# First-layer modulation as columns in the transposed copies, reordered loads, warmed roots, and a closing group by halves

## The chip, the cores and the metric

The kernel is one launch on one core of a Trainium2 chip. The metric is the device time in microseconds of that core. Three runs of the kernel before gave a median of 2481.85 us (2481.49 to 2483.36). All arithmetic is in float32.

PE is the tensor engine, DVE the vector engine, ACT the scalar (activation) engine, POOL the engine that issues the indirect gathers and the small loads, and SP the engine that issues nearly all the other loads. Each engine works its own instructions off in order and waits on semaphores.

## The reference

Two layers are computed over 256 latent tokens and 256 context tokens of width 1024. Layer 0 mixes tokens with multi-head latent attention (8 heads), layer 1 with grouped-query attention. After each mixer stands a PEER sub-layer: each token picks 16 of 16384 experts in each of 8 heads and takes their rows out of two tables. Cut to what matters here:

```python
for i in range(DEPTH):
    mod   = jax.nn.silu(c)     @ p['ada_w'] + p['ada_b']   # six parts of 1024
    mod_c = jax.nn.silu(c_ctx) @ p['ada_w'] + p['ada_b']
    h  = modulate(rmsnorm(x,  p['norm_mix']), sh_a,  sc_a)  # h * (1 + scale) + shift
    hc = modulate(rmsnorm(xc, p['norm_mix']), csh_a, csc_a)
    y, y_c = mixers[i % N_MIXERS](h, hc, *p['mixer'], need_ctx=need_ctx)
    x = x + g_a * y
    h = modulate(rmsnorm(x, p['norm_ffn']), sh_f, sc_f)
    x = x + g_f * peer_ffn(h, *p['peer'])
    if need_ctx: ...            # the same for the context, in layer 0 alone
return rmsnorm(x, norm_out)

# peer_ffn, a token and a head:
v1, i1 = top_k(s1, 16); v2, i2 = top_k(s2, 16)          # two lists of 128 keys
top_s, top_pos = top_k(v1[:, None] + v2[None, :], 16)   # of the 256 sums
expert = i1[pos // 16] * 128 + i2[pos % 16]
out += softmax(top_s) * gelu(t . u_tab[expert]) * v_tab[expert]
```

## The kernel before, in words

**Tiling.** A chunk is 128 tokens on the 128 partitions; chunks 0 and 1 are the context, 2 and 3 the latents. A *unit* is one chunk with one expert head. Layer 0 has 32 units (`FIRST`), layer 1 has 16. A unit has 16 gathers (L582), each of which brings for every token of the chunk one expert's row of both tables: 128 x 8 KB, 1 MB. DVE computes the dot product with the first half of a row (L2021), ACT applies Gelu and builds scaled diagonal matrices (L1256, L1553), and PE adds up the second halves through those diagonals into banks 0 to 3 of the accumulators (L1092). Units are worked in groups of four slots. The ring has 7, later 10, 12 and 15 slots. The rest of the latents' layer 0 (`lat`) is spliced between the groups at fixed positions.

**The opening.** Before the first gather, the context goes through the first attention and the modulation vectors of both layers are computed. The modulation weights are 48 pieces of 1 MB (`ada`); PE uses each with products into bank 0 (L141). Eight pieces make a *round*. The result of a round is 2 rows (latent and context) in each of four 32-partition groups; DVE adds the bias and folds in the norm gains (`ada_rows`, L1595 and L1607), POOL stores the rows in DRAM (L136), and where they are needed they are loaded again, broadcast over 128 partitions. For the first attention that is L545 (context) and L551 (latents), and `norm_rows` (L1611, L1612) scales and shifts a chunk by those rows before PE transposes it (`transposes`, L598) and ACT copies the transposed chunk out of the bank (`row_copies`, L1128). Then comes the input projection in two halves for each chunk (`in_half`, L603), and a loop over the 8 heads of the context (`ctx_proj`, `ctx_scores`, `ctx_transposes`, `ctx_values`), ten *turns* in all, each ended by three `ada` pieces. The output projection (`out_ctx`, L765) needs the weights `w_o_first`, which lie on slots 0 to 3 of the `ada` pieces; so the pieces from 35 on go through three slots only (`ada_place`, L274), one of which is the latent half of `hT`. Then follow the FFN norm, the first expert queries (L638), the scores, the two top-16 lists and `choose`, which ends with the indices of the first gather.

**Order of loads.** SP issues its loads in program order; a load into a slot in use waits for `ada_used`, and every later load waits behind it.

**The close of a chunk.** When the last group of a chunk's 8 units has been added up, DVE and ACT copy the four banks out (`add_output`, L1794 and L1795, and `copy_accumulators`), and DVE adds the result to x. That happens six times; behind the one at the end of layer 0 and the one at the end of the kernel no group follows at once.

**Roots.** Norms on ACT are a Square with accumulation and a Sqrt; the Sqrt needs a table load when Exp or Gelu came before (L1206, L1489).

## Time and profile before

| | |
|---|---|
| median of three runs | 2481.85 us |
| profiled execution, its time | 2484.57 us |
| profiled execution, its span | 2482.8 us |
| PE busy | 1669.9 us (67%) |
| DVE busy | 1587.5 us (64%) |
| ACT busy | 837.0 us (34%) |
| POOL busy | 922.7 us (37%) |
| gathers (software queue) | 811.23 MB, 79.4% of 16 engines' span |
| other loads and stores (hardware queue) | 119.50 MB, 13.0% |
| ACT table loads of the two largest groups | 86.0 and 61.6 us |

The span is from the first to the last instruction; the time of the same execution is 1.8 us longer. A busy share is an average over stages that are bound by different things, so the table says little by itself. The view in 40 slices of 62 us shows where the stages lie: slices 1 to 4 are the opening, slices 27 to 30 hold the end of layer 0 and the second attention, and all the others are units. "PEclk" is the granted clock of PE. The timeline lists instructions in order of time, with the idle time of the engine in front of each and what ended it; "x32" means that so many were merged in one row, and a float32 product appears there as two.

### The profile page before, as it was taken

The page shows a single profiled execution, that of the slowest core. Times are in us where ns is not written, and L with a number is a line of the kernel's source. Part 1 is how long each engine was busy: PE and PEld are TensorE (multiplying, and loading weights), DVE is VectorE, ACT ScalarE, POOL GpSimd, SP SyncE. Part 2 cuts the span into 40 slices and gives each one's busy share as a digit, 9 for nine tenths or more (in the row PEclk, how much of TensorE's full clock was granted, in tenths as well). Part 3 has the DMA queues.
Part 4 walks back from the last instruction along what each step waited for, and adds up shares of the span by engine and source line. Part 5 has one row for each costly group of instructions (what it writes and reads, how often), then busy time and mean ns, then how long its engine had stood idle before and what let it go on. Part 6 is the DMA issues. An engine that isn't in the chain of part 4 may idle for free. (4 is left out here: it accounts for less than half of the span.)

```text
span 2482.8 us, 27305 instructions
## 1 busy us (share of the span) xinstructions
PE 1669.9 (67%) x9121; PEld 727.2 (29%) x9121; DVE 1587.5 (64%) x3775; ACT 837.0 (34%) x2504; POOL 922.7 (37%) x836
## 2 busy tenths in 40 slices
PE   2988777777767667576755655568877565555554
PEld 0553543333324323232211211124543221111111
DVE  1132576788866667777777666544579687766654
ACT  1220334344452332434333433223333333332322
POOL 2010234444434444444444444410135444444440
PEclk8998898888888888888867867878989887777686
DMA  9895879999999999999999999982389999999995
GB/s 367 306 353 183 318 300 382 414 417 417 414 416 417 363 419 419 419 419 419 420 421 421 421 421 421 419 353 81 136 336 418 419 421 421 421 421 421 421 421 225
DMA packets 164974, 932.48 MB, mean 376 GB/s; under 512 B 16913, under 2 KB 51505, under 8 KB 60257
## 3 DMA queue, kind: packets, MB, share of 16 engines
q0 software_dynamic: 113392, 811.23, 79.4%
q1 hardware_dynamic: 51296, 119.50, 13.0%
q8 instruction: 72, 1.18, 0.2%
q14 instruction: 70, 0.57, 0.1%
q10 hardware_dynamic: 144, 0.01, 0.0%
HBM read 929.52 MB, written 1.15 MB: 375 GB/s over the span
## 5 line engine op out<-in xcount | busy, mean ns | idle before, releaser
L1092 PE MATMUL bank<-arena,aux 64*64 64x512 f32 x6144 | 989.8, 797 | 682.7 <-ACT aux L1553 653.3
L582 POOL DMA_INDIRECT arena<-in_uv,small x768 | 890.4, 1159 | 1331.6 <-PE bank L1092 959.8
L2021 DVE CUSTOM_DVE_ANT_0 arena<-arena,h 128x1024 f32<-128x1024 f32 x768 | 924.9, 1224 | 504.5 <-DMA arena<-in_uv,small 481.1
L1092 PEld LDWEIGHTS bank<-arena,aux 64*64 64x64 f32 x6144 | 281.6, 178 | 1337.3 <-ACT aux L1553 771.4
L1546 ACT ACTIVATE small<-small 128x4 f32<-128x4 f32 x192 | 39.3, 205 | 1201.4 <-DVE small L2021 1186.4
L1256 ACT ACTIVATE aux<-small 128x64 f32<-128x64 f32 x768 | 204.4, 336 | 8.9
L1553 ACT ACTIVATE aux<-aux,small 128x64 f32<-128x64 f32 x768 | 204.3, 336 | 6.5 <-issue 0.2
L638 PE MATMUL bank<-hT,aux 128*128 128x256 f32 (+1 forms) x768 | 170.2, 380 | 2.8 <-ACT hT L1128 2.8
L638 PEld LDWEIGHTS bank<-hT,aux 128*128 128x128 f32 x768 | 140.3, 203 | 49.0 <-issue 29.4
L1242 ACT ACT_TABLE_LOAD x67 | 86.0, 1283 | 1.2
L141 PE MATMUL bank<-arena,aux 128*32 128x512 f32 x312 | 48.3, 725 | 32.0 <-DMA arena<-in_ada 23.1
L136 POOL DMA_DIRECT2D mod_rows<-aux x24 | 12.1, 512 | 145.8 <-DVE aux L1607 90.1
L2021 DVE DVE_READ_ACCUMULATOR2_ANT small<- 128x1 f32 x768 | 62.9, 82 | 0.0
L1246 ACT ACT_TABLE_LOAD x48 | 61.6, 1283 | 0.8
L603 PE MATMUL bank<-arena,hT 128*128 128x384 f32 x128 | 45.5, 514 | 1.7 <-ACT arena L1295 1.1
L624 PE MATMUL bank<-arena 128*128 128x256 f32 x192 | 44.8, 383 | 0.9 <-ACT h L1320 0.9
L598 PE MATMUL bank<-ident,h 128*128 128x128 f32 x112 | 17.6, 308 | 39.9 <-DVE h L1612 39.9
L1755 DVE TENSOR_TENSOR aux<-small 128x256 f32<-128x256 uint32 x96 | 40.7, 424 | 4.7
L1757 DVE TENSOR_TENSOR aux<-aux,small 128x256 f32<-128x256 f32 x96 | 40.8, 426 | 3.3
L1758 DVE TENSOR_REDUCE small<-aux 128x16 f32<-128x256 f32 x96 | 40.3, 420 | 3.3
L1726 DVE MAX8 aux<-bank 128x8 f32<-128x128 f32 x84 | 25.0, 297 | 25.2 <-PE bank L646 11.4
L1123 ACT ACTIVATE h<-x 128x1024 f32<-128x1024 f32 x16 | 16.7, 1046 | 70.5 <-DVEq L1716 44.3
(224 smaller groups left out, 1519.3 us busy)
## 6 DMA issues: line engine op xcount, KB each, us to landing
arena<-in_ada SPq DMA_DIRECT2D x39, 1024.0 KB, 9.0
aux<-in_w_query SPq DMA_DIRECT2D x44, 512.0 KB
arena<-in_uv,small POOLq DMA_INDIRECT x768
hT<-in_ada SPq DMA_DIRECT2D x9, 1024.0 KB, 12.0
arena<-in_w_uq SPq DMA_DIRECT2D x16, 384.0 KB, 14.5
arena<-in_w_qkv SPq DMA_DIRECT2D x3, 2048.0 KB, 12.0
arena<-in_w_o SPq DMA_DIRECT2D x1, 4096.0 KB, 13.4
arena<-in_w_o SPq DMA_DIRECT2D x2, 2048.0 KB, 15.6
```

Source lines behind the costliest of these rows:

```text
L141: last = self.nc.tensor.matmul(bank[s * Q:(s + 1) * Q, :], self.cs[:, k, :], weights[:, 2 * s:2 * s + 2, :], start=(k == 0), stop=(k == KD ...
L582: nc.gpsimd.indirect_dma_start(out=ring[:, pos, :], out_offset=None, in_=d["uv"][unit // FIRST], in_offset=bass.IndirectOffsetOnAxis(ap=se ...
L603: last = nc.tensor.matmul(b[:, 0:HALF], hT[:, k, c * P:(c + 1) * P], self.w_in[:, k, half * HALF:(half + 1) * HALF], start=(k == 0), stop= ...
L624: last = nc.tensor.matmul(b[:, half * 256:half * 256 + 256], wq_head[:, k, half * P:half * P + P], cT[:, k, at:at + 256], start=(k == 0), ...
L638: last = nc.tensor.matmul(Q_BANK[:, side * 256 + at:side * 256 + at + width], weights[:, k, :], hT[:, k, lo:lo + width], start=(k == 0), s ...
L1092: last = nc.tensor.matmul(bank[2 * r + m][out:out + 64, :], self.dg[rr, (s + o) % 8, :], ring[rr, at, cols], start=first, stop=last_one)
L1242: nc.scalar.activation(self.warm, self.iota[:, 0:1], ACT.Gelu).then_inc(warmed, 1)
L1246: nc.scalar.activation(self.gate[:, m % 4, :], self.top, ACT.Exp, bias=self.nb, accum_out=self.es).then_inc(gate_done, 1)
L1256: last = nc.scalar.mul(self.gid[:, k, :], self.ident2, self.gate[:, m % 4, g * GRP + k:g * GRP + k + 1])
L1553: nc.scalar.mul(self.dg[:, s % 8, :], self.gid[:, k % GRP, :], self.w[:, n % 2, k:k + 1]).then_inc(diag_ready, 1)
L1757: link(nc.vector.tensor_tensor(self.OH, self.OH, self.indf[:, side, :].unsqueeze(1).broadcast_to([P, TOPK, TOPK]), ALU.mult))
L2021: last = nc.vector.tensor_tensor_reduce(out=ring[:, at, 0:D], in0=ring[:, at, 0:D], in1=h[:, c * D:(c + 1) * D], scale=1.0, scalar=0.0, op ...
```

## The change

1. **First attention's scale and shift as columns.** Chunks are only multiplied by their reciprocal root (ACT, `first_rows`), and transposed. The finished rows of round 0 are transposed on PE in four pieces, the useful columns are copied to `M0`, and the copies of the transposed chunks apply scale and shift per partition: four columns of a chunk on ACT (`first_copies`), four on DVE. The loads of these rows (L545, L551) and the four calls of `norm_rows` are gone. The latents' chunks are scaled in turn 4 of the head loop and copied by ACT, eight columns each, in the first units.
2. **Rows on two partitions.** Bias and gain rows are loaded to 2 partitions of each group instead of 32; the tiles are set to zero first.
3. **Loads reordered.** x comes in two halves, the latent half behind the first two heads' weights. `w_in` and `w_o` come by columns, in halves with a semaphore each. The first 8 `ada` pieces have a slot each. `w_o` is loaded after piece 28 instead of 34, when piece 25 has been used.
4. **PE's order.** Turns 8 and 9 of the loop use two pieces each, and the last six pieces are used between the output projections. The second half of chunk 1's output goes to bank 7 instead of bank 0.
5. **One-hot work at once.** `choose` handles both sides in three operations of 512 elements instead of six of 256.
6. **The closing group by halves.** In the last group of a chunk PE waits for all four diagonals and adds the first 512 output columns of all four slots, signals `closed`, then the other 512. The copies of the first half wait for `closed` alone.
7. **Warmed roots.** A Sqrt of a dummy tile stands ahead of the waits of four norms: the one behind layer 0's last chunk, layer 1's two FFN norms, and the last output norm.

The core of the diff:

```diff
-            eng.dma_start(rows[s * Q:(s + 1) * Q], bias[s].broadcast_to([Q, 512])).then_inc(loaded, 16)
+            eng.dma_start(rows[s * Q:s * Q + 2], bias[s].broadcast_to([2, 512])).then_inc(loaded, 16)
...
         def ada_place(n):
 
-            return n % 7 if n < 35 else 4 + (n - 35) % 3
+            return n if n < 8 else (n - 8) % 7 if n < 29 else 4 + (n - 29) % 3
...
+                sp.dma_start(x[:, CC:], d["tokens"][:, CC:]).then_inc(x_lat_loaded, 16)
...
-                    if n == 34:
-                        sp.wait_ge(ada_used, 32)
-                        sp.dma_start(self.w_o_first, d["w_o0"]).then_inc(w_o_loaded, 16)
+                    if n == 28:
+                        sp.wait_ge(ada_used, 26)
+                        for i in range(2):
+                            sp.dma_start(self.w_o_first[:, :, 512 * i:512 * i + 512], d["w_o0"][:, :, 512 * i:512 * i + 512]).then_inc(w_o_loaded[i], 16)
...
+                pe.wait_ge(rows_done, 1)
+                for j in range(4):
+                    last = nc.tensor.transpose(bank[1][:, j * P:(j + 1) * P], rows[0][:, j * P:(j + 1) * P], ident[:])
+                last.then_inc(m0_done, 1)
+                pe.wait_ge(nt_copied, 4)
+                pe.wait_ge(nt_moved, 4)
...
-                    for n in range(18 + 3 * u, 21 + 3 * u):
+                    for n in range(14 + 3 * u, 17 + 3 * u) if u < H else range(22 + 2 * u, 24 + 2 * u):
                         ada(n)
...
+                            closing = n % H == H - 1 and g == NG - 1
+                            pe.wait_ge(diag_ready, s + 2 + 2 * (closing and half == 0))
...
+                            if closing and half == 0:
+                                last.then_inc(closed, 1)
+                            else:
+                                last.then_inc(slots_free, 2 if closing else 1)
...
+                def first_copies(c, banks, ks):
+
+                    for k in ks:
+                        act.wait_ge(nt_done, 2 * c + k // 4 + 1)
+                        nc.scalar.activation(hT[:, k, c * P:(c + 1) * P], banks[k // 4][:, k % 4 * P:k % 4 * P + P], ACT.Identity,
+                                             bias=first_column(c, 0, k), scale=first_column(c, 1, k)).then_inc(nt_copied, 1)
...
+                for c, b in ((0, bank[6]), (1, bank[4])):
+                    for k in range(4, KD):
+                        dve.wait_ge(nt_done, 2 * c + 2)
+                        nc.vector.tensor_scalar(hT[:, k, c * P:(c + 1) * P], b[:, k % 4 * P:k % 4 * P + P],
+                                                first_column(c, 1, k), first_column(c, 0, k), ALU.mult, ALU.add).then_inc(nt_moved, 1)
...
                 def copy_accumulators(c):
                     for m in range(2):
+                        act.wait_ge(slots_free, (c + 1) * H * TOPK // 2) if m else act.wait_ge(closed, c + 1)
...
+                copy_accumulators(len(ORDER) - 1)
+                warm_sqrt()
                 out_norm(5, 3)
```

Three places of the order follow, in which the lines of the kernel after are its own. On PE, from the first `ada` product to the second transposes of projected rows, the kernel before has:

```order
L141 MATMUL bank<-arena,aux 32x512 x24
L141 MATMUL bank<-hT,aux 32x512 x4
L141 MATMUL bank<-arena,aux 32x512 x4
L598 MATMUL bank<-ident,h 128x128 x8
L603 MATMUL bank<-arena,hT 128x384 x16
L598 MATMUL bank<-ident,h 128x128 x8
L141 MATMUL bank<-arena,aux 32x512 x8
L603 MATMUL bank<-arena,hT 128x384 x16
L609 MATMUL bank<-ident,aux 128x128 x6
```

and the kernel after:

```order
L141 MATMUL bank<-arena,aux 32x512 x24
L605 MATMUL bank<-ident,h 128x128 x8
L141 MATMUL bank<-hT,aux 32x512 x4
L605 MATMUL bank<-ident,h 128x128 x8
L141 MATMUL bank<-arena,aux 32x512 x4
L695 MATMUL bank<-ident,aux 128x128 x4
L610 MATMUL bank<-arena,hT 128x384 x32
L141 MATMUL bank<-arena,aux 32x512 x8
L616 MATMUL bank<-ident,aux 128x128 x6
```

Both chunks are now transposed (L605) among the products of round 0, the rows of round 0 are transposed (L695) behind them, and the four halves of the projection (L610) stand together. On PE, the end of the head loop (`ctx_values`, L745) and the output projection (L765), before:

```order
L141 MATMUL bank<-arena,aux 32x512 x4
L745 MATMUL bank<-aux,arena 128x256 x2
L141 MATMUL bank<-arena,aux 32x512 x4
L141 MATMUL bank<-hT,aux 32x512 x4
L141 MATMUL bank<-arena,aux 32x512 x4
L765 MATMUL bank<-arena,hT 128x512 x24
L598 MATMUL bank<-ident,h 128x128 x8
```

and after (L760 and L782):

```order
L760 MATMUL bank<-aux,arena 128x256 x2
L141 MATMUL bank<-hT,aux 32x512 x4
L141 MATMUL bank<-arena,aux 32x512 x4
L782 MATMUL bank<-arena,hT 128x512 x16
L141 MATMUL bank<-arena,aux 32x512 x4
L141 MATMUL bank<-hT,aux 32x512 x4
L141 MATMUL bank<-arena,aux 32x512 x4
L782 MATMUL bank<-arena,hT 128x512 x8
L141 MATMUL bank<-arena,aux 32x512 x4
L141 MATMUL bank<-hT,aux 32x512 x4
L141 MATMUL bank<-arena,aux 32x512 x4
L605 MATMUL bank<-ident,h 128x128 x8
```

Six pieces moved behind the first two output projections. On SP, the loads around w_o, before:

```order
L400 DMA arena<-in_ada 128x2048 x3
L405 DMA arena<-in_w_uq 128x3x256
L406 DMA arena<-in_w_uk 128x2x128
L400 DMA hT<-in_ada 128x8x256
L442 DMA arena<-in_w_o 128x8192
L400 DMA arena<-in_ada 128x2048 x2
L400 DMA hT<-in_ada 128x8x256
```

and after:

```order
L410 DMA arena<-in_ada 128x2048
L410 DMA hT<-in_ada 128x8x256
L454 DMA arena<-in_w_o 128x8x512 x2
L410 DMA arena<-in_ada 128x2048
L415 DMA arena<-in_w_uq 128x3x256
L416 DMA arena<-in_w_uk 128x2x128
L410 DMA arena<-in_ada 128x2048
L410 DMA hT<-in_ada 128x8x256
```

The last head's weights (`w_uq`, `w_uk`) now follow w_o instead of preceding it, and nineteen pieces come behind it where thirteen did.

## Rows read from the trace of the kernel before

**Rows 1.** The page, 40 slices: ACT's busy tenths, and GB/s of all transfers.

```profile
ACT  1220334344452332434333433223333333332322
GB/s 367 306 353 183 318 300 382 414 417 417 414 416 417 363 419 419 419 419 419 420 421 421 421 421 421 419 353 81 136 336 418 419 421 421 421 421 421 421 421 225
```

**Rows 2.** The page, costliest groups: busy us, mean ns, idle before with its releaser.

```profile
L2021 DVE CUSTOM_DVE_ANT_0 arena<-arena,h 128x1024 f32<-128x1024 f32 x768 | 924.9, 1224 | 504.5 <-DMA arena<-in_uv,small 481.1
```

**Rows 3.** Timeline, start to first projection: start, us, engine, what, idle before.

```profile
31.91 1.93 PE L141 MATMUL bank<-hT,aux 128*32 128x512 f32 x8 [1.05 <-DMA hT<-in_ada]
34.39 1.81 PE L141 MATMUL bank<-arena,aux 128*32 128x512 f32 x8 [0.55 <-DMA arena<-in_ada]
37.10 0.69 DVE L1607 SCALAR_TENSOR_TENSOR aux<-aux 64x512 f32<-64x512 f32 x1
55.57 1.28 DVE L1611 SCALAR_TENSOR_TENSOR h<-x,small,arena 128x1024 f32<-128x1024 f32 x1 [17.78 <-DMA arena<-mod_rows]
60.88 13.44 PE L603 MATMUL bank<-arena,hT 128*128 128x384 f32 x32 [0.68 <-ACT hT L1128]
```

**Rows 4.** The timeline, second pair of projections to the head loop.

```profile
76.98 10.59 PE L603 MATMUL bank<-arena,hT 128*128 128x384 f32 x32
88.15 2.78 PE L141 MATMUL bank<-arena,aux 128*32 128x512 f32 x24
104.80 2.75 PE L624 MATMUL bank<-arena 128*128 128x256 f32 x12
```

**Rows 5.** The timeline, two starts of a turn, and the release of w_o.

```profile
135.25 0.69 PE L726 MATMUL bank<-aux 128*128 128x256 f32 x2
144.65 0.70 PE L726 MATMUL bank<-aux 128*128 128x256 f32 x2
153.31 0.33 SPq L442 DMA_DIRECT2D arena<-in_w_o  x1
```

**Rows 6.** The head loop's end: timeline, SP's waits, a window, DMA issues.

```profile
155.97 8.01 SPq L400 DMA_DIRECT2D arena<-in_ada  x2
210.42 22.35 PE L765 MATMUL bank<-arena,hT 128*128 128x512 f32 x48
...
SPq L400 <- PE bank L141: 109.1, 35, 15.3
...
175.00:180.00 5.00, 5.00 (x34) 3.23 (x37) 0.00 (x0) 1.47 (x6) 0.00 (x0) 1.00 0.37 149
...
hT<-in_ada SPq DMA_DIRECT2D x9, 1024.0 KB, 12.0
```

**Rows 7.** The timeline, transposes for the first query, and the first gather.

```profile
233.02 1.09 PE L598 MATMUL bank<-ident,h 128*128 128x128 f32 x8 [0.25 <-DVE h L1612]
251.36 1.02 POOL L582 DMA_INDIRECT arena<-in_uv,small  x1 [36.80 <-DVEq L1762]
```

**Rows 8.** The page, costliest groups: one of the one-hot operations.

```profile
L1755 DVE TENSOR_TENSOR aux<-small 128x256 f32<-128x256 uint32 x96 | 40.7, 424 | 4.7
```

**Rows 9.** The timeline, four column copies on ACT in the second layer.

```profile
1679.07 1.50 ACT L1421 ACTIVATE hT<-bank,small 128x128 f32<-128x128 f32 x4 [2.28 <-PE bank L598]
```

**Rows 10.** The timeline, second attention: query rows, a table load, two transposes.

```profile
1664.60 14.00 PE L971 MATMUL bank<-arena,hT 128*128 128x512 f32 x32
1736.91 1.28 ACT L1206 ACT_TABLE_LOAD   x1
1741.24 1.09 PE L598 MATMUL bank<-ident,h 128*128 128x128 f32 x8 [1.70 <-DVE h L1612]
1809.18 1.97 PE L598 MATMUL bank<-ident,h 128*128 128x128 f32 x8 [8.05 <-DVE h L1612]
```

**Rows 11.** The timeline, the tail: last products, first copy, table load.

```profile
2460.87 6.30 PE L1092 MATMUL bank<-arena,aux 64*64 64x512 f32 x32 [3.72 <-ACT aux L1553]
2467.25 0.69 DVE L1794 COPY aux<-bank 64x512 f32<-64x512 f32 x1 [7.29 <-PE bank L1092]
2475.25 1.28 ACT L1489 ACT_TABLE_LOAD   x1
```

More of the change, by code:

```diff
@@ L250, in trunk @@
         ring = v(self.arena, 0, 15, 2 * D)
-        ada_slots = [v(self.arena, i * ADA, KD, 256) for i in range(6)] + [hT[:, :, CTX:]]
+        ada_slots = [v(self.arena, i * ADA, KD, 256) for i in range(6)] + [hT[:, :, CTX:], v(self.arena, 20480, KD, 256)]
         rows = [self.aux[:, 6784:7296], self.aux[:, 0:512]]
@@ L353, in q_count, with a_count @@
             return 2 * j + 1 + side
+        def a_count(c, half):
+            return CC * half + c + 1 if c < CC else 2 * c + half + 1
         def entry(m):
@@ L428, in _ @@
                 sp.dma_start(self.rope_cols, d["rope_cols"][:, 0:CTX]).then_inc(small_loaded, 16)
-                for n in range(8, 11):
+                for n in range(8, 10):
                     ada(n)
@@ L433, in _ @@
                 head(1, False)
-                for n in range(11, 15):
+                sp.dma_start(x[:, CC:], d["tokens"][:, CC:]).then_inc(x_lat_loaded, 16)
+                for n in range(10, 14):
                     ada(n)
@@ L676, in _ @@
                 pe.wait_ge(silu_done, 1)
-                for n in range(KD):
+                for n in range(6):
                     ada(n)
@@ L703, in _ @@
                 an_transposes(an_ctx[:, 1], (bank[5], bank[6]))
-                for n in range(14, 18):
+                for n in range(12, 14):
                     ada(n)
@@ L771, in _ @@
                 out_ctx(0, 1)
+                for n in range(42, 45):
+                    ada(n)
                 out_ctx(1, 0)
+                for n in range(45, steps):
+                    ada(n)
                 pe.wait_ge(hf_ready, 1)
@@ L1082, in _ @@
                                     pe.wait_ge(added, NC + CC if n else CC)
-                            pe.wait_ge(diag_ready, s + 2)
-                            first, last_one = n % H == 0 and k == 0, n % H == H - 1 and k == TOPK - 2
-                            for m in range(2):
+                            closing = n % H == H - 1 and g == NG - 1
+                            pe.wait_ge(diag_ready, s + 2 + 2 * (closing and half == 0))
+                            first = n % H == 0 and k == 0
+                            for m in range(2) if not closing else (half,):
                                 cols = slice(D + 512 * m, D + 512 * m + 512)
-                                for o in range(2):
-                                    at = self.place[s + o]
+                                for o in range(2 if not closing else GRP):
+                                    slot = n * TOPK + g * GRP + o if closing else s + o
+                                    at = self.place[slot]
                                     for r in range(2):
                                         rr = slice(64 * r, 64 * r + 64)
-                                        out = 64 * (r ^ o)
-                                        last = nc.tensor.matmul(bank[2 * r + m][out:out + 64, :], self.dg[rr, (s + o) % 8, :], ring[rr, at, cols], start=first, stop=last_one)
-                            last.then_inc(slots_free, 1)
+                                        out = 64 * (r ^ (o % 2))
+                                        last = nc.tensor.matmul(bank[2 * r + m][out:out + 64, :], self.dg[rr, slot % 8, :], ring[rr, at, cols], start=first,
+                                                                stop=closing and o >= 2)
+                            if closing and half == 0:
+                                last.then_inc(closed, 1)
+                            else:
+                                last.then_inc(slots_free, 2 if closing else 1)
                             if half == 0:
@@ L1242, in warm_gelu, with warm_sqrt @@
                     nc.scalar.activation(self.warm, self.iota[:, 0:1], ACT.Gelu).then_inc(warmed, 1)
+                def warm_sqrt():
+                    act.wait_ge(warmed, warms[0])
+                    warms[0] += 1
+                    nc.scalar.activation(self.warm, self.iota[:, 0:1], ACT.Sqrt).then_inc(warmed, 1)
                 def gates(m):
@@ L1700, in _ @@
                         ctx_out(u - 2)
[L1701 to L1705 removed]
+                    if u == 2:
+                        first_mean(1)
+                    if u == 3:
+                        first_rstd(1)
+                    for r in range(1, LAYERS * ADA_ROUNDS - 1):
+                        if u == (0, 0, 3, 5, 8)[r]:
                             ada_rows(r)
```

208 lines of the change are left out of this document (110 added, 98 removed).

## The prediction

> **What bounds the kernel now.** I read the 40 slices first. For most of the span the transfers run at 414 to 421 GB/s [rows 1]: each of the 768 gathers brings 1 MB, DVE's dot products stand idle 481 us for them [rows 2], and an engine made faster there is worth nothing. The transfers are below that pace in three stretches: before the first gather at 251 us (slices 1 to 5), in the second attention (slices 27 to 30, down to 81 GB/s), and in the tail. Whatever is taken out of those stretches moves every later gather forward, so the sum is made there and carried through.
>
> The opening read in order of time has four parts. First, the modulation rows of round 0 are ready at 37.79, are stored and loaded back broadcast, are read at 55.57, and the input projection `in_half` starts only at 60.88: 26.5 us from the last modulation product, in which PE does nearly nothing [rows 3]. Second, the projections and value rows until the head loop at 104.80 [rows 4]. Third, the head loop, which PE fills: a turn is 144.65 - 135.25 = 9.4 us, three products with the modulation weights among it [rows 5]. Fourth, from the release of w_o at 153.31, what waits is PE for modulation weights: they come through three slots, SP waits 109 us in all for PE to give slots back, and between 175 and 180 the transfers fall to 149 GB/s because no slot is free [rows 6]. So the opening is bound by a round trip first, by PE in the middle, and by slots and transfers at its end.
>
> **The change, part by part, against the profiled execution** (span 2482.8, time 2484.57; the median of the runs is 2481.85, 2.7 less, and I take the gain off both).
>
> 1. Columns instead of the round trip. In front of the eighth modulation piece, the queue loses the latent half of x (1.05 MB) and most of twelve 64 KB row loads (0.79 MB, now 0.05). Two pieces land 34.39 - 31.91 = 2.48 us apart [rows 3], so 1.8 MB is 4.2 us, and the piece is used at 30.2. From there to finished rows is the 3.4 us of before (37.10 + 0.69 - 34.39): 33.6. Then four transposes (at most the 1.09 of eight, [rows 7]), the copy of the columns with its waits (0.7), and four column copies on ACT, 1.50 [rows 9], beside four on DVE: the projection starts at about 37.0, 23.9 us earlier. Its weights come 1.6 MB, 3.8 us, behind the eighth piece, at 34, so they are hidden; if they weren't, the second half waits to 38 behind two projections of 5.3 us and more. The four new memsets hold POOL's row loads back by a microsecond or two, beside transfers that last to 30. Bounds: 20 if nothing of the 4.2 comes, 25.
> 2. The four projections run back to back: 13.44 + 10.59 = 24.0 [rows 3, 4], to 61.0 against 87.57, since the transposes of chunk 1 no longer stand between them. To the head loop it was 104.80 - 87.57 = 17.2, with eight modulation products behind the projections; now six stand there, 2 x 0.93 less [rows 4]: 76.3.
> 3. w_o is released after turn 3, not 4. 48.5 us less a turn, 39.1. Added are one reload of Exp behind the latent Sqrt, 1.28 [rows 10], in ACT's chain to the next scores, and places where a product waits for rows in turns 0 and 3; I take 1.9 for all (0 to 4). The two squares and two scalings of latent rows are hidden: ACT is busy for 2 tenths of the slice in which these turns lie [rows 1]. Release at 117.3, 36.0 earlier.
> 4. From the release to the first output projection it took 210.42 - 153.31 = 57.1, for w_o and thirteen pieces. The same thirteen (29 to 41) stand there now, and one more head's 0.5 MB: 58.4, to 175.7. Low bound: 19.4 MB at the 406 of the full stretches would be 48 plus landing, 50; high bound 62.
> 5. Six pieces are used behind the output projections instead of ahead: six products of 0.93 and about 1 us of waiting for their landing are added to 22.35 [rows 6]: 29 (28 to 34). The transposes of 233.02 come at 204.7.
> 6. From them to the first gather 18.34 [rows 7], less one-hot work: six operations of 256 elements, 0.42 to 0.43 us each [rows 8], become three of 512 at about 0.7: 0.6 less. First gather at 222.4, 28.9 earlier (bounds 20 and 38). POOL's last store lies behind ada rows that end near 206, and its landing is over before 222; wq and the keys are issued at about 190.
> 7. The ring of seven slots after it. ACT copies 8 columns per latent chunk, 3.0 us for 1.1, twice; DVE saves 0.6 a unit. PE is the busy engine there and neither stands alone in its way. I take 0, bounds +4 and -4.
> 8. Second layer. At its start PE computes query rows for 14.0 us while the rows are normalised [rows 10], so the halves and the first warmed Sqrt gain nothing, and PE starts its closing group 0.5 later because it waits for four diagonals: 0. At the first FFN norm the load of 1.28 lies in a PE wait of 1.70, at the second in one of 8.05 [rows 10]: 1.28 each, plus 0.6 of one-hot work ahead of the gathers: 3.2 less. With the 0.5, 2.7.
> 9. Tail. The load of 1.28 goes. The 32 products of 6.30 become two halves [rows 11]; DVE's first two of four copies of 0.69 lie beside the second half, less the 0.5 of the later start: 0.9. In all 2.2.
>
> Here a page differs from the row. The row has 1.28 us for a table load, in both places [rows 10, 11]. The Trainium skill (ScalarE: Activation LUTs, What ACT_TABLE_LOAD costs) puts a drain of 1.38 us beside the load, 2.66 in all. By it the three loads taken off would give 4 us more; the trace shows no row of 1.38 beside it, and the sum stays with the row.
>
> Sum: 28.9 + 2.7 + 2.2 = 33.8. Of the profile's 2484.57 that leaves 2450.8, of the median 2448.
>
> **Rivals.**
> A, supply. If the opening were paced by bytes alone, only the bytes taken out would count: four broadcast rows of 0.52 MB and 32 row loads of 64 KB, 4.2 MB, 10 us at the pace of rows 3. With 4.9 of the later parts: 2467. For it: transfers at 367 GB/s in the first slice [rows 1]. Against it: 306 in the second and 183 in the fourth, and 149 in the stretch of rows 6; those are gaps, not a full pipe.
> B, room. If the pieces come at the low bound of step 4 and step 5 stays at 28: nine more, 2440. For it: PE has one more turn to do after w_o's release with pieces already in place. Against it: the three slots.
> C, slower. The three-slot ring begins at piece 29 instead of 35 and carries nineteen pieces instead of thirteen. Before, thirteen took 54.4 us (155.97 to 210.42), 4.2 each [rows 6]. At that pace nineteen from about 124 (the release and 6.6 us of the turn's other work) end at 204, which agrees with step 5. The median landing in the hT slot is 12.0 us [rows 6]; if it, the product and 6.6 us of a turn's other work never overlapped, a round of three would take 19.5, nineteen pieces 123, and the transposes would come at 248: 15 later, less the 4.9: about 2492. It decides from 5.9 us per piece, up from 4.2. Against it: that round was 12.6 before with the same work beside it.
> D, given back. First gather early, but the seven-slot stage longer by the same, because ACT's column copies stand before PE's projections: it would take 29 us where 4 are added: 2479.
>
> **How the numbers follow.** My case 0.68, A 0.14, B 0.10, C 0.05, D 0.03. The likeliest gives 2449 (its own range 2441 to 2457). The range 2436 to 2466 takes in B, nearly A and the bounds of steps 3 to 7. A run tells 0.2%, 5 us, from no change: faster 0.92 (my case, A, B), within it 0.03 (D), slower 0.05 (C).
>
> **What would show it.** `in_half` starts near 37 and no load of modulation rows stands before it; the head loop starts near 76; w_o goes out near 117; the first output projection starts near 176; the first gather is issued near 222. No table load between the squares and the root at 1737, 1805 and the end (in their new places). The slices of the gathers stay at 414 to 421. It is wrong if w_o's release comes early but the output projection doesn't (C), if PE waits for w_in or for pieces 8 to 15 (A), or if the gathers of slices 4 to 7 take longer than before (D).

## The result and the profile after

The changed kernel takes 2450.52 us (median of four runs, 2448.89 to 2456.11) against 2482.61 (2481.49 to 2485.47): a ratio of 0.9879, 95% interval 0.9864 to 0.9894. The forecast was 2449, range 2436 to 2466. The profiled execution took 2451.81, its span 2450.0 against 2482.8: 32.8 us less, where the sum said 33.8. The total came out so close partly because its terms erred both ways.

The page of the changed kernel, to be laid beside [rows 1]: ScalarE's busy tenths and the transfers.

```profile
ACT  2312433344533423434333523233332323332322
GB/s 382 309 353 248 308 308 402 415 418 419 414 416 367 410 419 418 419 419 418 421 421 421 421 422 421 420 350 57 151 371 418 419 421 421 421 421 421 421 421 235
```

Slice 4 went from 183 to 248, slice 7 from 382 to 402, and the full stretches stand at 414 to 422, where it was 414 to 421: nothing was won while the gathers run, all of it ahead of them and between them.

The opening in order of time (start, us, engine and operation, idle before it), against [rows 3 to 7]:

```profile
27.88 1.06 PE L141 MATMUL bank<-arena,aux 128*32 128x512 f32 x8
29.83 0.69 DVE L1663 SCALAR_TENSOR_TENSOR aux<-aux 64x512 f32<-64x512 f32 x1
31.27 0.22 DVE L1716 COPY small<-bank 128x64 f32<-128x64 f32 x1 [0.75 <-PE bank L695]
31.52 2.90 ACT L1192 ACTIVATE hT<-bank,small 128x128 f32<-128x128 f32 x8 [13.56 <-DVE small L1716]
33.08 22.43 PE L610 MATMUL bank<-arena,hT 128*128 128x384 f32 x64 [1.85 <-ACT hT L1192]
69.85 2.75 PE L631 MATMUL bank<-arena 128*128 128x256 f32 x12
...
116.51 1.25 SPq L454 DMA_DIRECT2D arena<-in_w_o  x2
...
178.09 14.00 PE L782 MATMUL bank<-arena,hT 128*128 128x512 f32 x32
205.43 1.09 PE L605 MATMUL bank<-ident,h 128*128 128x128 f32 x8
223.24 1.01 POOL L589 DMA_INDIRECT arena<-in_uv,small  x1 [13.25 <-DVEq L1832]
```

No load of modulation rows stands between the rows of round 0 and the projection, which starts 27.8 us earlier. The head loop starts 35.0 earlier, w_o goes out 36.8 earlier, the first output projection comes 32.3 earlier and the first gather 28.1.

In the second attention and in the tail the Sqrt load has moved off the chain. Again the changed kernel's timeline, against [rows 10, 11]:

```profile
1702.79 1.28 ACT L1293 ACT_TABLE_LOAD   x1
1713.38 1.09 PE L605 MATMUL bank<-ident,h 128*128 128x128 f32 x8 [0.61 <-DVE h L1668]
...
2430.69 6.16 PE L1114 MATMUL bank<-arena,aux 64*64 64x512 f32 x32 [4.13 <-ACT aux L1608]
2434.45 0.69 DVE L1864 COPY aux<-bank 64x512 f32<-64x512 f32 x1 [5.15 <-PE bank L1114]
...
2438.13 1.28 ACT L1293 ACT_TABLE_LOAD   x1
2438.56 1.23 DVE L1868 TENSOR_TENSOR aux<-aux,arena 128x1024 f32<-128x1024 f32 x1
```

The load at 2438.13 now lies beside VectorE's sums, and the first copy starts 3.8 us after the products' start where it was 6.4.

### The profile page after: what moved, and what is told of

Same layout as the page of the kernel before. It is cut to its first block and busy times, and to the rows that moved or that the text cites. A ratio compares the mean times of both kernels' runs of the same rounds, so it can differ in the third digit from the quotient of the medians.

```text
span 2450.0 us, 27206 instructions
## 1 busy us (share of the span) xinstructions
PE 1657.0 (68%) x9125; PEld 720.5 (29%) x9125; DVE 1560.5 (64%) x3635; ACT 849.0 (35%) x2530; POOL 933.8 (38%) x832
## 5 line engine op out<-in xcount | busy, mean ns | idle before, releaser
L589 POOL DMA_INDIRECT arena<-in_uv,small x768 | 903.0, 1176 | 1292.4 <-PE bank L1114 965.0
L1601 ACT ACTIVATE small<-small 128x4 f32<-128x4 f32 x192 | 39.3, 205 | 1206.2 <-DVE small L2090 1206.1
L1297 ACT ACT_TABLE_LOAD x48 | 61.6, 1283 | 0.9
L610 PE MATMUL bank<-arena,hT 128*128 128x384 f32 x128 | 44.5, 507 | 3.0 <-ACT hT L1192 3.0
L1740 DVE TENSOR_TENSOR aux<-bank,aux 128x256 f32<-128x256 f32 x16 | 6.8, 425 | 53.6 <-ACT aux L1216 44.6
L631 PEld LDWEIGHTS bank<-arena 128*128 128x128 f32 x192 | 35.8, 190 | 11.4 <-issue 6.1
L1825 DVE TENSOR_TENSOR aux<-small 128x512 f32<-128x512 uint32 x48 | 33.1, 691 | 3.1
L1827 DVE TENSOR_TENSOR aux<-aux,small 128x512 f32<-128x512 f32 x48 | 33.3, 693 | 1.6
L1828 DVE TENSOR_REDUCE small<-aux 128x32 f32<-128x512 f32 x48 | 32.9, 686 | 1.6
## 6 DMA issues: line engine op xcount, KB each, us to landing
arena<-mod_rows SPq DMA_DIRECT2D x7, 512.0 KB, 22.3
```

The costliest lines, as they stand in the source:

```text
L589: nc.gpsimd.indirect_dma_start(out=ring[:, pos, :], out_offset=None, in_=d["uv"][unit // FIRST], in_offset=bass.IndirectOffsetOnAxis(ap=se ...
L610: last = nc.tensor.matmul(b[:, 0:HALF], hT[:, k, c * P:(c + 1) * P], self.w_in[:, k, half * HALF:(half + 1) * HALF], start=(k == 0), stop= ...
L631: last = nc.tensor.matmul(b[:, half * 256:half * 256 + 256], wq_head[:, k, half * P:half * P + P], cT[:, k, at:at + 256], start=(k == 0), ...
L1297: nc.scalar.activation(self.gate[:, m % 4, :], self.top, ACT.Exp, bias=self.nb, accum_out=self.es).then_inc(gate_done, 1)
L1601: nc.scalar.activation(self.w[:, n % 2, ks], self.a[:, n % 2, ks], ACT.Gelu).then_inc(gelu_done, 1)
```

## The experiments

Twelve kernels were run, all of them edits of the changed one. Runs of one kernel differ by up to 11 us (bytes, 2456.38 to 2467.33), so each is read first in its profile: at the head loop's start, at w_o, at the first output projection and at the first gather. The table has these, the time of the profiled execution that they come from, and the median; 69.85, 116.51, 178.09 and 223.24 are those of the changed kernel.

The marks come from one execution each, and they scatter too. The changed kernel, nowarm, whole and plain have the same instructions in the opening, yet from the head loop's start they took 107.9 to 110.6 us to the output projection and 153.1 to 157.3 to the first gather. A mark that moves by less than 3 to 4 us shows nothing by itself. Nor is the profiled execution always a typical one: take's and best's were the fastest of theirs (take's by 5 us), lat's and all3's the slowest (all3's by 5).

| kernel | head loop | w_o | output | gather | profiled us | median us | ratio to before, interval |
|---|---|---|---|---|---|---|---|
| roundtrip | 89.56 | 136.11 | 200.44 | 245.49 | 2473.29 | 2473.29 | 0.9962 (0.9948 to 0.9976) |
| rows32 | 72.66 | 119.31 | 185.54 | 232.28 | 2457.29 | 2457.34 | 0.9901 (0.9886 to 0.9916) |
| bytes | 76.84 | 123.50 | 187.30 | 233.30 | 2459.14 | 2458.83 | 0.9910 (0.9885 to 0.9935) |
| wolate | 70.31 | 144.42 | 177.55 | 223.35 | 2452.16 | 2452.20 | 0.9877 (0.9860 to 0.9893) |
| take | 68.00 | 109.98 | 173.01 | 218.74 | 2446.30 | 2451.65 | 0.9881 (0.9864 to 0.9897) |
| lat | 70.35 | 115.75 | 179.51 | 224.63 | 2456.08 | 2451.21 | 0.9870 (0.9854 to 0.9887) |
| parts | 70.06 | 101.48 | 176.12 | 223.49 | 2448.88 | 2448.79 | 0.9873 (0.9856 to 0.9889) |
| all3 | 70.92 | 102.76 | 175.07 | 221.82 | 2451.30 | 2445.99 | 0.9856 (0.9840 to 0.9873) |
| nowarm | 69.77 | 116.43 | 177.67 | 222.85 | 2453.94 | 2455.23 | 0.9900 (0.9876 to 0.9923) |
| whole | 70.35 | 116.62 | 180.96 | 227.28 | 2448.77 | 2452.18 | 0.9883 (0.9868 to 0.9898) |
| plain | 70.61 | 117.01 | 180.36 | 227.90 | 2450.24 | 2451.70 | 0.9879 (0.9861 to 0.9898) |
| best | 69.76 | 101.18 | 170.74 | 216.05 | 2441.51 | 2444.21 | 0.9847 (0.9834 to 0.9861) |

**roundtrip** gives the context rows their way over memory back. The transposes of both chunks stand behind these rows again, and the transposed chunks are copied plainly. Cut to what matters:

```diff
+ for j, seg in enumerate((SC_A, SH_A)):
+     pool.dma_start(self.mix_rows[:, j], self.mod_row(0, CON, seg)).then_inc(ctx_rows_loaded, 16)
...
- for stage in range(3):        # stage 2 scales the context chunks
+ for stage in range(2):
...
+ for c in range(CC):
+     norm_rows(c, self.mix_rows[:, 0], self.mix_rows[:, 1], h_ready)
```

> The changed kernel with the context rows of the first input projection scaled and shifted as before: GpSimd loads scale and shift back from memory as broadcast rows, VectorE applies them to whole rows, and the transposed rows are copied plainly; the columns are still made, for the latent rows. Theory (the round trip was on the path, as steps 1 to 4 have it): rows done at 30.5, in_half starts 20 to 23 us later than 33.1, the head loop, w_o's release and the first output projection each move by the same, and the time is 2469 to 2474. Rival A (the opening is paced by bytes): in_half starts as late, but only the 1 MB of broadcast rows counts by the first output projection, which moves by under 6 us; time 2453 to 2457.

```profile
47.81 1.28 DVE L1670 SCALAR_TENSOR_TENSOR h<-x,small,arena 128x1024 f32<-128x1024 f32 x1 [15.03 <-DMA arena<-mod_rows]
50.41 1.97 PE L607 MATMUL bank<-ident,h 128*128 128x128 f32 x8 [17.89 <-DVE h L1671]
54.41 1.78 PE L612 MATMUL bank<-arena,hT 128*128 128x384 f32 x5
...
200.44 2.84 PE L784 MATMUL bank<-arena,hT 128*128 128x512 f32 x6
```

VectorE waits 15.03 us for the rows and TensorE 17.89 for VectorE. The projection starts 21.3 later, the output projection 22.3, the first gather 22.2, and the time is 22.8 higher. What is lost at the start is lost at the end, one for one. That is the larger part of the change's 32, and rival A is gone.

**bytes** and **rows32** put the bytes ahead of the eighth piece back, both edits or the rows alone.

```diff
- eng.dma_start(rows[s * Q:s * Q + 2], bias[s].broadcast_to([2, 512])).then_inc(loaded, 16)
+ eng.dma_start(rows[s * Q:(s + 1) * Q], bias[s].broadcast_to([Q, 512])).then_inc(loaded, 16)
...                              # the gains the same; in bytes alone, behind the context half of x:
+ sp.dma_start(x[:, CC:], d["tokens"][:, CC:]).then_inc(x_lat_loaded, 16)
```

> The changed kernel with the bytes in front of the eighth modulation piece put back: each row of the biases and gains is again loaded for 32 partitions (64 KB, was 4 KB), and the latent half of x stands right behind the context half. Theory (step 1: 4.2 us of the 23.9 come from these bytes): the last product of round 0 runs 4 to 5 us later than 27.9, in_half starts near 37.5, and everything behind moves by as much; time 2453 to 2456. Rival: the transfers had slack ahead of the eighth piece, which moves by under 2 us; time 2450 to 2452.

> The changed kernel with only the row loads put back to 32 partitions (64 KB each, was 4 KB); x stays in two halves. The two edits together cost 6.2 us at the eighth modulation piece. Theory 1 (bytes): twelve rows of 64 KB are 0.79 MB, at the pace of the pieces (1 MB in 2.48 us) 1.9 us; the latent half of x has the rest. Theory 2 (the row loads slow the transfers beside them: with them the transfers ran near 300 GB/s between 8 and 17 us, without them near 420): they alone cost 3.5 to 4.5 us, in_half starts at 36.5 to 37.5. Time 2452.5 by theory 1, 2454 to 2455 by theory 2.

The last product of round 0 ran at 34.04 and at 31.70, against 27.88: the two edits are worth 6.2 us there (4 to 5 were expected), the rows alone 3.8, twice what their 0.79 MB would take at the pieces' pace. In bytes the projection starts at 39.71, where 37.5 was expected, and the median is 8.3 us higher, where 3 to 6 were. The transfers between 8 and 18 us show why. First the kernel before, then the changed one, then rows32; after the total stand one queue's packets, MB and share of engine time.

```profile
DMA packets 646, 3.08 MB, mean 308 GB/s; under 512 B 205, under 2 KB 205, under 8 KB 363
...
q1 hardware_dynamic: 329, 2.43, 82.3%
```

```profile
DMA packets 1050, 4.20 MB, mean 420 GB/s; under 512 B 403, under 2 KB 531, under 8 KB 551
...
q1 hardware_dynamic: 702, 4.15, 99.8%
```

```profile
DMA packets 810, 3.00 MB, mean 300 GB/s; under 512 B 236, under 2 KB 364, under 8 KB 541
...
q1 hardware_dynamic: 451, 2.27, 75.0%
```

In those 10 us the row loads don't only take their own 0.7 MB: the total falls from 420 to 300 GB/s. With 82.3% of the engines' time the pieces' queue moved 2.43 MB in the kernel before, 0.295 MB per us of full share, and 0.416 in the changed one. Theory 2 holds at the eighth piece. The time is 6.8 higher where 3.5 to 4.5 were expected, and where the other 3 us come from is open. From the release of w_o to the output projection rows32 took 66.2 us and the changed kernel 61.6, but bytes, with the same row loads, took 63.8, and whole and plain, without them, 64.3 and 63.4: that the row loads of later rounds cost anything isn't shown.

**wolate** keeps seven slots until piece 32 and loads w_o behind piece 35.

```diff
- return n if n < 8 else (n - 8) % 7 if n < 29 else 4 + (n - 29) % 3
+ return n if n < 8 else (n - 8) % 7 if n < 33 else 4 + (n - 33) % 3
- if n == 28: sp.wait_ge(ada_used, 26)
+ if n == 35: sp.wait_ge(ada_used, 33)
```

> The changed kernel with w_o loaded behind piece 35 instead of piece 28: the ring keeps its seven slots until piece 32, and w_o waits for piece 32. Theory (steps 3 to 5: from w_o's release to the first output projection the time is that of w_o and the pieces through three slots, so an earlier release is worth most of what it is earlier): w_o goes out near 145 instead of 116.5, the waits of 4.38 to 1.06 us for pieces 29 to 31 go, but w_o and the pieces behind it land later, the first output projection starts 3 to 8 us later than 178.1; time 2453 to 2458. Rival C's mechanism in small (three slots from piece 29 on cost more than an early w_o brings): the first output projection starts no later than 178, time 2445 to 2450.

```profile
144.42 1.26 SPq L454 DMA_DIRECT2D arena<-in_w_o  x2
161.73 1.93 PE L141 MATMUL bank<-arena,aux 128*32 128x512 f32 x8 [11.44 <-DMA arena<-in_ada]
...
177.55 2.91 PE L782 MATMUL bank<-arena,hT 128*128 128x512 f32 x3
```

w_o goes out 27.9 us later, and the output projection starts half a microsecond earlier. My theory failed here. SP's wait ahead of w_o is 16.5 us in wolate and 15.5 in the changed kernel: the loads stand still for a slot about as long in either, and where they do made no difference. The waits for pieces moved with it (one of 11.44 at 161.73 in place of 4.38, 2.89 and 1.06 at 137.75 to 144.79), and up to the output projection their sum stayed: 14.9 us against 14.6.

**take** lets VectorE empty the bank of round 2 earlier in turn 3, **lat** takes the latent rows' norm (ScalarE's part and VectorE's), and with it two table loads, out of the turns.

```diff
  ctx_maxima(u)
+ if u == 3:
+     ada_rows(2)        # was: behind rotate, ctx_out and first_rstd
```

```diff
+ for stage in range(3):
+     first_rows(1, stage)     # behind an_scale of chunk 1
- if 2 <= u < 5: first_rows(1, u - 2)
```

> The changed kernel with one step of VectorE moved: in turn 3 of the first attention it adds the third round of modulation products out of their bank right behind the maxima of the scores, and no longer behind the rotated query part, which there waits for ScalarE's reloaded Exp. Theory (the turn was the mis-sized term): the wait of TensorE of 3.94 us at 112.82 falls to under 1.5, the products behind it run at the fast clock, w_o goes out 4 to 6 us before 116.5, the first output projection and the first gather come 3 to 6 us earlier, and the time is 2445 to 2447 against 2450.5. Rival (ScalarE's reload alone is what costs): the wait stays because the products have nothing else to run on, and the gain is under 1 us.

> The changed kernel with the squares, the root and the two scalings of the latent rows taken out of turns 2 to 4 and put behind the second normalisation of the context, where the Sqrt table is loaded: two table loads go out of the turns. Theory: turn 3 shrinks by the reload of 1.28 us and by what stands behind it on ScalarE and VectorE, so TensorE's wait of 3.94 at 112.82 falls to 1 to 2, and w_o goes out 3 to 5 us before 116.5; nothing is lost between 58 and 70, since TensorE computes value rows there; time 2446 to 2448. Rival: the work delays the copies of the value rows and the head loop starts 2 to 4 us later, so the time stays at 2450.

The mis-sized turn of the changed kernel:

```profile
107.82 1.07 PE L141 MATMUL bank<-arena,aux 128*32 128x512 f32 x8
107.98 0.59 ACT L1232 COPY aux<-bank 128x512 f32<-128x512 f32 x1 [5.83 <-PE bank L760]
108.58 1.28 ACT L1225 ACT_TABLE_LOAD   x1
...
111.05 0.39 ACT L1218 COPY aux<-bank 128x256 f32<-128x256 f32 x1
...
111.26 0.42 DVE L1740 TENSOR_TENSOR aux<-bank,aux 128x256 f32<-128x256 f32 x1 [7.20 <-ACT aux L1216]
112.01 0.67 DVE L1651 TENSOR_TENSOR aux<-aux,bank 128x512 f32<-128x512 f32 x1
...
112.82 3.64 PE L141 MATMUL bank<-arena,aux 128*32 128x512 f32 x16 [3.94 <-DVE aux L1651]
```

Piece 23 is the last of round 2, so piece 24 needs the bank emptied. VectorE is to do that at 112.01, behind a copy that waits for ScalarE, which reloads Exp. TensorE idles 3.94 us, and its next 16 products take 3.64; the granted clock is 0.50 (1.2 GHz) from 112 to 116.5. In take, where they take 1.92, it is 1.00 from 108 to 110:

```profile
106.73 1.28 ACT L1225 ACT_TABLE_LOAD   x1
...
107.17 0.69 DVE L1651 TENSOR_TENSOR aux<-aux,bank 128x512 f32<-128x512 f32 x1 [4.96 <-PE bank L141]
...
108.00 1.92 PE L141 MATMUL bank<-arena,aux 128*32 128x512 f32 x16 [0.97 <-DVE aux L1651]
```

The same reload now leaves TensorE idle for 0.2 us at most: its next product follows at 110.09. From the head loop's start to w_o it takes 42.0 us instead of 46.7. In lat, without the reload, the wait is still 2.46 and that stretch 45.4. So VectorE's order was the cause, and the reload only made it longer. The wait and the slow products account for take's 4.7 us: 3.0 less waiting, 1.7 less in the products. Of them 3.2 seem to arrive at the output projection (105.0 from the head loop's start for 108.2, and under the 107.9 to 110.6 of the four like kernels) and 2.6 at the gather; lat brings nothing there. By time neither is told from the changed kernel: 2451.65 where 2445 to 2447 were expected, and 2451.21 where 2446 to 2448 were.

**parts** loads w_o by its four slots, and **all3** has all three edits.

```diff
- sp.wait_ge(ada_used, 26)
- for i in range(2):
-     sp.dma_start(self.w_o_first[:, :, 512 * i:512 * i + 512], ...)
+ for i in range(4):
+     sp.wait_ge(ada_used, 23 + i)
+     sp.dma_start(self.w_o_first[:, 2 * i:2 * i + 2], ...)   # the first output projection waits for all four
```

> The changed kernel with w_o of the first attention loaded in four parts of 1 MB by heads, each as soon as its own slot has been used (after pieces 22 to 25), where it was two halves that both wait for piece 25. Theory (the transfers stand idle between about 104 and 117 because every slot waits): two parts, 2 MB, go out before 110, so that pieces 29 to 31 land about 5 us earlier, the waits of 4.38, 2.89 and 1.06 us at 137.8 to 144.8 mostly go, and the first output projection starts 3 to 5 us before 178.1; time 2446 to 2448. Rival (from there on the three slots pace it, a piece is loaded only when another was used): the waits go but come back at the later pieces, the output projection moves by under 1.5 us.

> The three edits together (VectorE's early add, w_o in four parts, latent rows earlier). Theory: the turn term is given back once (5 to 6 us, the first and third edits have the same wait), w_o's parts bring 3 to 5 more; the first output projection starts near 168 to 171, the first gather near 214 to 217; time 2441 to 2445. Rival (slots pace everything behind the release): the gain is that of the turn alone, 2445 to 2447.

In parts the transfers between 100 and 120 rise from 158 to 305 GB/s, the output projection comes 2.2 us sooner after the head loop's start, and the first gather not at all (153.4 in either). The gap closed at 110 opens again between 140 and 160 (261 GB/s), so its rival was nearer. What was still ahead at the output projection went in that block itself: its first 32 products took 14.00 us in the changed kernel and 15.96 in parts. The windows over the two blocks, the changed kernel first; the number before the DMA share and the GB/s is the granted clock.

```profile
178.00:193.00 15.00, 15.00 (x48) 6.38 (x48) 2.15 (x4) 0.00 (x0) 0.00 (x0) 1.00 0.41 148
```

```profile
176.00:192.00 16.00, 16.00 (x36) 6.80 (x32) 1.38 (x2) 0.00 (x0) 0.00 (x0) 0.87 0.34 114
```

all3 misses its marks at the output projection and the gather (175 and 222 for 168 to 171 and 214 to 217), with a head loop that began 1.1 late, the output block at a granted clock of 0.88, and a profiled execution 5 us over its other three. Its median of 2445.99 is the rival's; that behind the release the slots pace it fits this, and isn't shown by it.

**nowarm** leaves the four dummy roots out, **whole** computes the closing groups undivided.

```diff
- warm_sqrt()        # in four places
```

```diff
- closing = n % H == H - 1 and g == NG - 1
+ closing, last_one = False, n % H == H - 1 and k == TOPK - 2   # and no copy waits for `closed`
```

> The changed kernel without the four dummy square roots that load the Sqrt table ahead of a norm. Theory (steps 8 and 9): nothing at the start of the second layer, 1.28 us at its first and 1.28 at its second FFN norm, 1.1 to 1.28 in the tail; the stretch from the end of the first layer's groups to those of the second is 2.5 us longer, and the tail 1.1: 3.6 us in all, time about 2454. Rival (the wait of TensorE that the first FFN norm lengthens also drops its clock for the query products, which took 5.24 us before and 3.84 after): 1.4 us more, 5 in all. Rival by the page's drain of 1.38 us beside each load: 6 to 7.

> The changed kernel with each closing group of products computed as before, column half beside column half in two rounds of 16, and copied when all are done. Theory (step 9): in the tail the first two copies no longer lie beside the second half of the products, from the last dots to the end 0.9 to 1.4 us more; at the start of the second layer TensorE starts 0.5 us earlier and the query rows hide the rest, nothing or a gain of 0.5. Time 2451 to 2452. Rival: TensorE's start of the group, which waits for two diagonals and not for four, comes 0.5 us earlier and gives back half of it in the tail, under 0.6 in all.

In nowarm the transposes of the first latent FFN norm wait longer, and so do those of the second (8.05 for 6.96):

```profile
1714.68 1.09 PE L605 MATMUL bank<-ident,h 128*128 128x128 f32 x8 [1.71 <-DVE h L1664]
1716.50 3.84 PE L645 MATMUL bank<-hT,aux 128*128 128x128 f32 x32 [0.73 <-ACT hT L1154]
```

That is 1.1 each, and 1.1 in the tail (from the first sum to the reciprocal 6.5 for 5.4): 3.3 by the waits. By the whole stretch, from the last Gelu of the first layer to the first of the second, it is 161.2 us for 159.3, so 1.9 for the two, and 3.0 in all; the second query products happened to run faster in nowarm (5.18 us for 6.61, at a granted clock of 0.73 for 0.56). A load of 1.28 costs 1.09 here, because part of it lies beside VectorE's step, for which the Sqrt without a load waits 0.2 us. The first query products take 3.84 with and without warming, at a granted clock of 1.00. In the kernel before they were slower:

```profile
1743.06 5.24 PE L638 MATMUL bank<-hT,aux 128*128 128x128 f32 x32 [0.73 <-ACT hT L1128]
```

The granted clock there was 0.71. So the load and the longer wait don't bring the 5.24 back, and that rival falls. No drain shows up. The Trainium skill (ScalarE: Activation LUTs, What ACT_TABLE_LOAD costs) would make it 2.66 each, and the runs don't agree. (By the expectation's own figures three such drains come to 3.6 + 4.1 = 7.7 us, not 6 to 7; either is far from 3.3.) The median rose by 4.7, which with runs that scatter by more contradicts neither 3.0 nor 3.3.

Between whole and nowarm the closing products took the same 5.09 us, so their tails compare: from the last Gelu to VectorE's first sum 9.04 undivided and 8.15 in halves, 0.9 by the division. At the start of the second layer nothing changes (159.1 against 159.3 us from the last Gelu of the first layer to the first of the second).

**plain** copies the latent chunks without columns; it leaves their scale and shift out of the computation.

```diff
- first_copies(2, lower, range(KD))
+ plain_copies(2, lower)       # two copies of 4 x 128, no scale, no shift; chunk 3 the same
```

> The changed kernel with the latent chunks copied plainly behind their transposes, in two copies of 512 columns each instead of eight with scale and shift; it leaves the scale and the shift of the latent rows out of the computation. After the change the groups of the first ring drift back from 28.9 to 26.4 us earlier between the first and the 24th. Theory (ScalarE's column copies stand ahead of TensorE's projections and of the diagonals): those 2 us come back, most of them by the eighth group, time 2448. Rival (the drift is the meeting of the ring with the transfers, which run full from the twelfth group on): nothing moves by over 0.5 us, time 2450 to 2451.

It settles nothing. From the first output projection to the 13th group of dots the kernel before took 224.8 us, the changed one 229.9, plain 227.4, but whole, which has the column copies, 226.8. In plain and whole the first gather came 4 us late, and their 13th group, at 407.7 each, no later than the changed kernel's at 408.0. That first stage of the ring swallows some microseconds by itself, and the columns' part in it is below what these runs tell. The median, 2451.70 for the 2448 of the theory, says no more.

**best** joins take and parts and spreads the pieces of turns 6 to 9.

```diff
  if u < H: ctx_scores(u)
+ if u >= 6: ada(pieces.pop(0))
  if u + 1 < H:
      ctx_proj(u + 1)
+     if u >= 6: ada(pieces.pop(0))
```

> VectorE's early add and w_o in four parts, and from turn 6 on the three modulation products of a turn spread over it (one behind the scores, one behind the projections, the rest at its end), where they stood together at its end: each slot comes free at another time of the turn, so the transfers, at 260 to 280 GB/s between 140 and 160, have something to do. Theory: waits for pieces in turns 6 to 9 (1.90, 1.68, 1.32, 1.41 us after the change) mostly go, the first output projection starts at 170 to 174, the first gather at 216 to 219, time 2443 to 2446. Rival: a product that waits in the middle of a turn holds the projections and the chain through ScalarE and VectorE, and the turn is no shorter: time as without the spreading, 2446 to 2448.

```profile
159.73 1.06 PE L141 MATMUL bank<-arena,aux 128*32 128x512 f32 x8 [1.55 <-DMA arena<-in_ada]
166.23 1.93 PE L141 MATMUL bank<-hT,aux 128*32 128x512 f32 x8 [2.91 <-DMA hT<-in_ada]
...
170.74 4.56 PE L787 MATMUL bank<-arena,hT 128*128 128x512 f32 x10
...
216.05 1.01 POOL L589 DMA_INDIRECT arena<-in_uv,small  x1 [13.26 <-DVEq L1839]
```

Output projection at 170.7, 4.3 ahead of all3 (3.2 from the head loop's start), first gather at 216.05, and 2444.21 us (2441.51 to 2445.21): all five runs lie below all four of the changed kernel, and both marks and the time lie where they were expected. The waits for pieces in turns 6 to 9 did not mostly go, though: 4.5 us are left of 6.3. The transfers between 140 and 160 still run at 290 GB/s, which fits slots that still bind, but wasn't tested. This version beats both kernels; its ratio to before is 0.9847 (0.9834 to 0.9861). From all3 it isn't told by time: all3's interval is 0.9840 to 0.9873.

## Why the prediction was right, and where it was not

**Steps 1 and 2** had the mechanism, and roundtrip shows it. The projection started 27.8 us earlier, where 25 was the high bound, since each size was taken on the cautious side. The bytes ahead of the eighth piece were put at 4.2 us by the pieces' pace; bytes measures 6.2, since the wide row loads slow the transfers beside them. From the eighth piece to finished rows it took 2.6 us, not 3.4, and from there to the projection 2.6, not 3.4. From the projection to the head loop 36.8 us were needed, not 39.3; 1.6 of these 2.5 are the block of 64 products (22.43 for 24.0), whose length changed between executions with the clock. The head loop began 6.5 us earlier than forecast.

**Step 3** lost nearly all of that again. The stretch of 41.0 us took 46.7. The term "1.9 for all (0 to 4)" was the one mis-sized: it held the reload and a wait for rows, but not that VectorE empties the bank behind a copy which waits for the reload. With that put right take measures 42.0. So the release came at 116.5 for 117.3 by two errors that cancelled.

**Step 3 to 4 as a cause** was wrong though the numbers held. I hung the output projection on w_o's release; wolate moves the release by 28 us and nothing follows. The release was a mark on TensorE's way through the turns, and roundtrip shows that it is the start of those turns which carries through. **Step 4** itself took 61.6 against 58.4. The stretch from the release to the output projection in the kernel before, then in the changed one (length, busy time of PE, of its weight loads, of DVE, ACT and POOL, then granted clock, DMA share, GB/s):

```profile
153.31:210.42 57.11, 40.80 (x221) 20.14 (x221) 11.34 (x26) 6.39 (x21) 6.06 (x12) 0.88 0.96 353
```

```profile
116.51:178.09 61.58, 46.86 (x252) 26.16 (x252) 12.28 (x28) 8.23 (x27) 11.09 (x22) 0.88 0.93 341
```

TensorE's waits for pieces add up to 14.8 us in the first and 14.6 in the second, so it is not waiting that the term missed. TensorE works 6.1 us more, because one more turn of the head loop now lies in the stretch, and a wait of 1.6 for VectorE is gone. Step 4 counted transfers alone and put that turn at nothing. (Its low bound took 406 GB/s for the full stretches, which show 414 to 421 in [rows 1]; that moves its 48 us to 46 or 47 and nothing else.) **Step 5** was 27.3 for 29, **step 6** 17.8 for 17.7, and the first gather came at 223.2 for 222.4.

**Step 7**, taken as 0 with bounds of 4, lost 2.5: the first group of dots was 28.9 earlier, the 17th 26.6, and so it stayed within 1.3 to the end of the layer. Its cause stays open.

**Step 8** brought 4.1 for 2.7 (26.6 earlier at the query rows of the second attention, 30.7 at the last dots). The two loads are 1.1 each by their waits; 1.4 are query products that took 3.84 us for 5.24 at a granted clock of 1.00 for 0.71, which was in no term. nowarm shows that it isn't the warming's doing; it came out alike in all the kernels with the change, and which part of the change brings it is open. The rest is the one-hot work, 3 x 0.69 for 6 x 0.42, which is 0.45 where the sums took 0.6. **Step 9** brought 2.1 for 2.2.

Rival A falls by roundtrip, as a pace for the whole opening; in front of the eighth piece bytes do count, and more than their size. C falls by wolate: to begin with three slots earlier neither cost nor brought anything. B falls by the waits for pieces that still stand. D did not happen in its size; by its own terms its price was 2477, not 2479 (2481.85 less the 4.9 of the later parts).

## What to carry to other kernels

A mark that moves together with the end is not yet its cause: before a chain is hung on a transfer's release, move that release alone. Where a bank or a slot passes from one engine to the next, look at what stands ahead of the emptying step in its engine's order, because a reload elsewhere is harmless until somebody waits behind it. Small loads that spread one row over many partitions are to be charged with what they take from the transfers beside them, not with their bytes.

## What the runs showed of the hardware

Row loads of 64 KB beside 1 MB pieces brought the total down from 420 to 300 GB/s between 8 and 18 us, although they moved 0.7 MB of 3.

Why they take that much is open: the profile has the shares, not the reason. The rule nearest to it is on transfer size (the Trainium skill, Perfetto Trace Analysis, DMA Optimizations: small transfers under 2 KB have a significant overhead each). The trace doesn't bear it out as the reason here. In the slow stretches there were fewer packets under 2 KB than in the fast one (205 in the kernel before and 364 in rows32, against 531).

The block of 64 projection products came out at different lengths from the same instructions: 20.91 us in take, 22.43 in the changed kernel, 23.90 in all3, where the granted clock between 30 and 70 us was 1.00, 0.96 and 0.91. It starts at 32.7 to 33.1 in all three. That is up to 3 us from one profiled execution to another, in a block that no edit touched; an edit of a few microseconds in the opening is therefore to be read from the head loop's start on, and even behind it the output block moves by 2 us in the same way (14.00 and 15.96). Whether it is why the runs of the changed kernel spread over 7 us was not tested.
